# Adding the convolution's four channel chunks on VectorE before the mean product of an encoder layer

## The chip, the cores and the metric

The kernel runs on one core of a Trainium2 chip. The metric is the device time of one execution in microseconds (us); lower is better. The kernel before took 1318.83 us, the median of three runs that lay between 1318.5 and 1320.07 us.

## The reference

One encoder layer on 512 tokens of 1024 features. Two branches run on the normalised input and are joined by an output projection; a mixture of 32 experts (four for each token) follows, and a last norm. The part that the change touches is the layer norm of the convolution branch:

```
def conformer_conv(a, g, conv_w, conv_b, ln_g, ln_b):
    u = a * jax.nn.sigmoid(g)
    u = lax.conv_general_dilated(u, conv_w[:, None, :], ..., feature_group_count=D_CONV) + conv_b   # 31 taps, 512 channels
    uf = u.astype(jnp.float32)
    mu = jnp.mean(uf, axis=-1, keepdims=True)                   # over the 512 channels
    var = jnp.mean(jnp.square(uf - mu), axis=-1, keepdims=True)
    un = (uf - mu) * lax.rsqrt(var + EPS) * ln_g + ln_b
    return jax.nn.silu(un)
...
mixed = jnp.concatenate([conv_out, na_out], axis=-1)
return jnp.einsum("bse,ed->bsd", mixed, w_out) + b_out
```

The other branch, `na_out`, is attention with 8 heads of 64 over a neighbourhood of the 8 by 64 grid of tokens.

## The kernel before

The engines run programs of their own, written out by hand, and meet at semaphores. The work comes in stages: norm and input projection, convolution, attention, output projection, second norm and routing, then a loop over the experts, and the final sum and norm. The expert loop streams 12 pieces of 1 MB of weights for each expert; ScalarE and VectorE split each piece into a high and a low part, and TensorE multiplies. A piece's buffer is loaded again once TensorE has used it.

The convolution is done by VectorE. The 512 channels lie in four chunks of 128 partitions, `mixedT[:, c, :]`, each 128x512 f32. A tap is one instruction over a chunk (line 1190), 31 for each chunk, 124 in all. 88 of them are made before the attention; the last 36 lie two by two behind the scores of attention steps 0 to 17 (`TAP_STEPS`). The taps go round among the first two chunks that are not complete, and each waits for the one before it on its chunk.

The attention has 32 steps, `i` from 0 to 31: four blocks of 128 queries by 8 heads. In step `i`:

- VectorE (lines 1287 to 1314): `scores(i)` adds the bias table to the products and takes the row's extreme (line 1247); two taps; at steps 10, 18, 26 and 34 `normalise(n)` comes first, a reciprocal (line 1276) and a division of the block's output (line 1281), which waits for TensorE's value products `pv` of the 8 steps before. At steps 19 to 22 a chunk is centred (line 1302), which waits for `mean_done`.
- ScalarE: the exponential of step `i` (line 813) and the copy of the transposed weights (line 761).
- TensorE (lines 1911 to 1935): `transpose_p(i)` (line 1854), which waits for the exponential; in even steps `qk_pair(i + 4)`, the score products of two steps ahead (line 1844), which wait for `s_ready`; `pv(i - 1)` (line 1865). The first `pv` of a block waits for `normalise` of the block before (`o_ready`).

The mean over the channels is a product of a 128x128 matrix filled with 1/512 (`mean_w`) with each chunk, accumulated in bank 5 (line 1926), behind `pv` of steps 14, 15, 17 and 18. Each f32 product is two matmul instructions in the profile. `MEAN_OF` gives the places. Centring, squares (line 858, added up at line 1308), the product for the variance (line 1932) and the transposes of the next block's output at step 23 follow in this order. The output projection begins with `project_attn(1)` (line 1886) once the last `pv` is issued.

Of the kernel before, what the change touches and what calls it, by code (L numbers as in the profile page):

```python
# [10 lines left out]
ALU = mybir.AluOpType  # L11
# [18 lines left out]
CC = D_CONV // P  # L30
# [33 lines left out]
def encoder_kernel(nc, x, g_mix, w_in, b_in, conv_w, conv_b, ln_g, ln_b, rpb, w_out, b_out,  # L64
# [3 lines left out]
    with ctx:  # L68
        def sem(name):
            return ctx.enter_context(nc.semaphore(name))  # L70
# [10 lines left out]
        def area(name, shape, dt=F32):  # L81
            at = free[0]
            size = int(np.prod(shape[1:])) * (2 if dt == BF16 else 4)
            free[0] = at + -(-size // 128) * 128 if name == "area_u" else at + -(-size // 32) * 32
            return nc.alloc_sbuf_tensor_at(name, shape, dt, offset=at), at
# [10 lines left out]
        area_a, a_at = area("area_a", [P, 4096])  # L96
# [76 lines left out]
        mixedT = area_m[:, 0:2048].rearrange("p (k t) -> p k t", k=CC)  # L173
# [8 lines left out]
        mask = area_m[:, 3072:3072 + 768]  # L182
        sq = area_u[:, 0:2048].rearrange("p (b t) -> p b t", b=CC)
        ln_rs = area_a[:, 1024:1536]

        convT_out = [area_u[:, 512 * c:512 * (c + 1)] for c in range(CC)]
        T_mid = area_t[:, 0:2048].rearrange("p (h t) -> p h t", h=HEADS)
# [74 lines left out]
        mean_w, mean_at = area("mean_w", [P, P])  # L262
# [29 lines left out]
        bank = [pair[i // 2][:, 512 * (i % 2):512 * (i % 2 + 1)] for i in range(8)]  # L292
# [35 lines left out]
        conv_tap = sem("conv_tap")  # L328
        tables_ready = sem("tables_ready")
        mean_done = sem("mean_done")  # L330
        centred = sem("centred")
        squared = sem("squared")
        var_done = sem("var_done")
# [21 lines left out]
        attn_low_ready = sem("attn_low_ready")  # L355
# [96 lines left out]
        WOUT_PARTS = ((1, 2), (1, 3), (0, 2), (0, 3), (1, 0), (1, 1), (0, 0), (0, 1))  # L452
        TAP_STEPS = 18
        CENTRE_AT, SQUARE_AT, TURN_AT = 19, 20, 23
        MEAN_OF, SQUARES_AT, VAR_AT = {14: 0, 15: 1, 17: 2, 18: 3}, {23: (0, 1), 25: (2, 3), 27: (0, 2)}, 29
        next_tap, last_tap = [0] * CC, [0] * CC
        steps = [(n, hd) for n in range(NQ) for hd in range(HEADS)]
        NS = len(steps)
# [1 line left out]
        def normalised_at(i, first):  # L460
            return (i - first) // HEADS if i >= first and (i - first) % HEADS == 0 and (i - first) // HEADS < NQ else None

        def turned_at(i, behind):
            at = [10, TURN_AT, 26, 34]
            return at.index(i - behind) if i - behind in at else None
# [645 lines left out]
        def _(dve):  # L1111
            v = nc.vector
# [82 lines left out]
            def taps(count, known=CC):  # L1195

                for _ in range(count):
                    left = [c for c in range(known) if next_tap[c] < CONV_K]
                    tap(min(left[0:2], key=lambda c: last_tap[c]))
# [42 lines left out]
            def scores(i):  # L1242
                n, hd = steps[i]
                dve.wait_ge(qk_done, i + 2 - i % 2)
                if i >= 3:
                    dve.wait_ge(exp_ready, i - 2)
                v.tensor_tensor_reduce(out=S_sb[:, i % 3, :], in0=bank[i % 4][:, 0:KEYS], in1=table_of(n, hd),
                                       scale=1.0, scalar=3.0e38, op0=ALU.add, op1=ALU.min,
                                       accum_out=neg_max[:, i:i + 1]).then_inc(s_ready, 1)
# [8 lines left out]
            def attn_low_part(n):  # L1258
                tokens = slice(n * P, (n + 1) * P)
                dve.wait_ge(attn_high_ready, 4 * (n + 1))  # L1260
                for c in range(4):
                    v.scalar_tensor_tensor(attn_low[:, c, tokens], bank[5][:, c * P:(c + 1) * P], colT[:, 16 + c:17 + c],
                                           attn_high[:, c, tokens].bitcast(F32), ALU.add, ALU.subtract).then_inc(attn_low_ready, 1)
# [9 lines left out]
            def normalise(n):  # L1273

                dve.wait_ge(exp_ready, HEADS * (n + 1))
                v.reciprocal(row_inv[:, n * HEADS:(n + 1) * HEADS], row_sum[:, n * HEADS:(n + 1) * HEADS]).then_inc(inv_ready, 1)
                dve.wait_ge(inv_ready, n + 1)
                dve.wait_ge(pv_done, HEADS * (n + 1))
                if n:
                    dve.wait_ge(o_transposed, n)  # L1280
                v.tensor_tensor(O_sb.rearrange("p (h d) -> p h d", d=HEAD_DIM),
                                bank[7][:, :].rearrange("p (h d) -> p h d", d=HEAD_DIM),
                                row_inv[:, n * HEADS:(n + 1) * HEADS].unsqueeze(2).to_broadcast([P, HEADS, HEAD_DIM]),
                                ALU.mult).then_inc(o_ready, 1)

            WOUT_AT = {24: 0, 26: 1, 28: 2, 30: 3}
            for i in range(NS + 6):
                n = normalised_at(i, 10)
                if n is not None:
                    normalise(n)  # L1290
                if i < NS:
                    scores(i)
                if i < TAP_STEPS:
                    taps(2)
                n = turned_at(i, 3)
                if n is not None:
                    attn_low_part(n)
                if CENTRE_AT <= i < CENTRE_AT + CC:
                    c = i - CENTRE_AT
                    dve.wait_ge(mean_done, 1)  # L1300
                    dve.wait_ge(conv_tap, CONV_K * CC)
                    v.tensor_tensor(mixedT[:, c, :], mixedT[:, c, :], bank[5][:, :], ALU.subtract).then_inc(centred, 1)
                if i in SQUARES_AT:
                    a, b = SQUARES_AT[i]
                    dve.wait_ge(squared, max(a, b) + 1)
                    if (a, b) == (0, 2):
                        dve.wait_ge(var_summed, 2)
                    v.tensor_tensor(sq[:, a, :], sq[:, a, :], sq[:, b, :], ALU.add).then_inc(var_summed, 1)
                if i in WOUT_AT:
                    wout_low_part(WOUT_AT[i])  # L1310
                if i == NS + 3:
                    dve.wait_ge(std_ready, 1)
                    for q in range(4):
                        v.reciprocal(ln_rs[:, q * P:(q + 1) * P], ln_rs[:, q * P:(q + 1) * P]).then_inc(ln_rs_ready, 1)
# [423 lines left out]
            for k in range(11, NJ):  # L1738
                if k in ADD_AT:
                    i = ADD_AT.index(k)  # L1740
# [40 lines left out]
        def _(pe):  # L1781
            t = nc.tensor
            pe.wait_ge(consts_ready, 9)

            for n in range(NQ):
                pe.wait_ge(xn_ready, n + 1)
                for half in range(2):
                    i = 2 * n + half
                    if i >= 4:
                        pe.wait_ge(xnT_low_ready, i - 3)  # L1790
                    for c in range(4):
                        k = 4 * half + c
                        last = t.transpose(bank[4 + i % 4][:, c * P:(c + 1) * P], xn_tile[:, n % 2, k * P:(k + 1) * P], ident[:, :])
                    last.then_inc(xn_transposed, 1)
                if n == 0:
# [4 lines left out]
                    last = t.transpose(bank[0][:, 32:32 + rows], stage[0:rows, 1, :], ident[0:rows, 0:rows])  # L1800
# [11 lines left out]
            for g in range(16):  # L1812
# [9 lines left out]
                for k in range(KD):  # L1822
                    last = three_products(bank[g % 4][:, :], high[:, k, :], low[:, k, :], xnT_high[:, k, :], xnT_low[:, k, :], k)
# [87 lines left out]
            for i in range(NS + 5):  # L1911
                if i < NS:
                    transpose_p(i)
                if i % 2 == 0 and i + 4 < NS:
                    qk_pair(i + 4)
                if 1 <= i <= NS:
                    pv(i - 1)
                n = turned_at(i, 0)
                if n is not None:
                    transpose_o(n)  # L1920
                if i in MEAN_OF:
                    c = MEAN_OF[i]
                    pe.wait_ge(conv_tap, last_tap[c])
                    if c == 0:
                        pe.wait_ge(attn_low_ready, 4)
                    last = t.matmul(bank[5][:, :], mean_w[:, :], mixedT[:, c, :], start=(c == 0), stop=(c == CC - 1))
                    if c == CC - 1:
                        last.then_inc(mean_done, 1)
                if i == VAR_AT:
                    pe.wait_ge(var_summed, 3)  # L1930
                    pe.wait_ge(s_ready, NS - 3)
                    t.matmul(bank[0][:, :], mean_w[:, :], sq[:, 0, :], start=True, stop=True).then_inc(var_done, 1)
                if i == NS + 1:
                    pe.wait_ge(s_ready, NS)
                    project_attn(1)
# [43 lines left out]
            for n in range(NQ):  # L1979
                for m in range(n + 1):  # L1980
                    last = t.matmul(bank[0][:, n * 32:(n + 1) * 32], (before_b if m == n else ones_b)[:, :], chosen[:, m, :],
                                    start=(m == 0), stop=(m == n))
            for m in range(NQ):
                last = t.matmul(bank[0][:, NQ * 32:NQ * 32 + 32], ones_b[:, :], chosen[:, m, :], start=(m == 0), stop=(m == NQ - 1))
# [3 lines left out]
            for n in range(NQ):  # L1988
                last = t.matmul(bank[1][0:CAP, 0:2], first_pos[:, n, :], first_tok[:, n, :], start=(n == 0), stop=(n == NQ - 1))
# [4 lines left out]
                     start=True, stop=True).then_inc(sorted_turned, 1)  # L1994
# [247 lines left out]
```

## Time and profile before

| | |
|---|---|
| median of three runs | 1318.83 us (1318.5 to 1320.07) |
| the profiled execution | 1317.1 us |
| its span | 1315.4 us |
| TensorE matmul busy | 1257.9 us, 96% |
| VectorE busy | 1225.4 us, 93% |
| ScalarE busy | 967.1 us, 74% |
| GpSimd busy | 319.3 us, 24% |
| mean granted TensorE clock | 0.984 of full speed |
| the mean's products, line 1926 | 8 matmul instructions, 167.3 to 178.0 us |

The profiled execution is one run with the profiler on. Its span goes from the first to the last instruction; the 1.7 us that its time has beside the span lie around the program. Busy time is the time in which an engine has an instruction under way, and where a group of instructions is given, overlapping ones count once.

### The profile page before, as it was taken

What the parts mean: (1) busy time and instruction counts of PE and PEld (TensorE: products, weight loads), DVE (VectorE), ACT (ScalarE), POOL (GpSimd) and SP (SyncE); (2) the same over time, 40 slices, a digit from 0 to 9 for tenths busy, and PEclk for the clock granted to TensorE, in tenths of its full rate; (3) what the DMA queues carried; (4) which work ended last, traced back from release to release, by engine and by line L of the source; (5) the groups of instructions that cost most, each with busy time, mean ns of one, the idle gap of its engine ahead of it and who ended that gap; (6) DMA issues with size and microseconds to landing.
All of it is one profiled execution on the core that took longest, in us unless ns stands there. A gap on an engine that the chain in (4) does not pass through costs nothing.

```text
span 1315.4 us, 17620 instructions
## 1 busy us (share of the span) xinstructions
PE 1257.9 (96%) x5713; PEld 1001.4 (76%) x5713; DVE 1225.4 (93%) x1028; ACT 967.1 (74%) x788; POOL 319.3 (24%) x245
## 2 busy tenths in 40 slices
PE   4999889789999999999999999999999999999986
PEld 4887668667878778787778788887887878778764
DVE  6799976689999999999999999999999999999997
ACT  4241665358797979888878888888979797979761
POOL 6001000101132313141404141332323222313153
PEclk9999889979999999999999999999999999999999
DMA  9925791589999999999999999999999999999995
GB/s 285 389 80 145 272 367 37 206 312 410 391 422 404 423 410 416 411 414 419 410 408 409 422 410 420 412 421 411 421 409 422 410 421 411 421 411 422 406 388 166
DMA packets 89961, 481.60 MB, mean 366 GB/s; under 512 B 11017, under 2 KB 11316, under 8 KB 40774
## 3 DMA queue, kind: packets, MB, share of 16 engines
q1 hardware_dynamic: 77742, 448.89, 84.7%
q0 software_dynamic: 10400, 27.14, 6.1%
q10 hardware_dynamic: 1784, 5.14, 1.2%
q8 instruction: 18, 0.29, 0.1%
q14 instruction: 17, 0.14, 0.0%
HBM read 447.46 MB, written 41.66 MB: 372 GB/s over the span
## 4 chain that ended last, share of the span: by engine, by line
PE 77%; DVE 15%; issue 4%; ACT 2%; DMA 1%; POOL 0%; SPq 0%; DVEq 0%; ACTq 0%; POOLq 0%
PE pair L2026 13%; PE pair L2027 12%; PE pair L2028 12%; PE pair L2042 10%; PE pair L2043 10%; DVE w_low L1347 4%; DVE area_m L1190 4%; PE pair L2013 2%; PE pair L2006 2%; PE pair L2040 2%; PE pair L2049 2%; PE pair L2061 2%; PE pair L1807 1%; PE pair L1808 1%; PE pair L1809 1%
## 5 line engine op out<-in xcount | busy, mean ns | idle before, releaser
L1347 DVE TENSOR_TENSOR w_low<-w_raw,w_high 128x2048 fp32r<-128x2048 f32 x380 | 836.2, 2243 | 28.0 <-ACT w_high L885 26.1
L885 ACT CAST w_high<-w_raw 128x2048 fp32r<-128x2048 f32 x380 | 700.8, 1875 | 159.1 <-PE pair L2028 126.1
L2042 PE MATMUL pair<-w_high,xS 128*128 128x512 f32 x488 | 198.9, 408 | 0.4 <-DVE w_low L1581 0.2
L2026 PE MATMUL pair<-w_high,xT_high 128*128 128x512 f32 x480 | 192.4, 401 | 1.5 <-DVE w_low L1347 1.5
L2043 PE MATMUL pair<-w_low,xS 128*128 128x512 f32 x488 | 190.6, 391 | 0.0
L2027 PE MATMUL pair<-w_low,xT_high 128*128 128x512 f32 x480 | 188.0, 392 | 0.0
L2028 PE MATMUL pair<-w_high,xT_low 128*128 128x512 f32 x480 | 187.4, 390 | 0.0
L2026 PEld LDWEIGHTS pair<-w_high,xT_high 128*128 128x128 f32 x480 | 90.1, 188 | 30.9 <-DVE w_low L1347 6.7
L664 POOL DMA_INDIRECT y_rows<-area_m,place_now x30 | 104.9, 3497 | 28.1 <-issue 28.1
L2042 PEld LDWEIGHTS pair<-w_high,xS 128*128 128x128 f32 x488 | 91.7, 188 | 24.3 <-issue 4.2
L2043 PEld LDWEIGHTS pair<-w_low,xS 128*128 128x128 f32 x488 | 91.8, 188 | 21.9 <-issue 3.8
L642 POOL CAST sel_in<-is_expert 128x128 fp32r (+1 forms) x16 | 46.9, 2934 | 242.1 <-PE pair L2043 242.1
L2026 PE MATMUL pair<-w_high,hT_high 128*128 128x512 f32 x256 | 102.1, 399 | 3.3 <-DVE w_low L1347 3.3
L2028 PEld LDWEIGHTS pair<-w_high,xT_low 128*128 128x128 f32 x480 | 90.2, 188 | 19.6
L2027 PEld LDWEIGHTS pair<-w_low,xT_high 128*128 128x128 f32 x480 | 90.2, 188 | 17.4
L2028 PE MATMUL pair<-w_high,hT_low 128*128 128x512 f32 x256 | 100.5, 393 | 0.0
L2027 PE MATMUL pair<-w_low,hT_high 128*128 128x512 f32 x256 | 100.5, 392 | 0.0
L2042 PE MATMUL pair<-w_high,hS 128*128 128x512 f32 x240 | 95.0, 396 | 0.0
L2043 PE MATMUL pair<-w_low,hS 128*128 128x512 f32 x240 | 93.5, 390 | 0.0
L1190 DVE SCALAR_TENSOR_TENSOR area_m<-area_u,convT,area_m 128x512 f32<-128x512 f32 x120 | 83.6, 745 | 0.4
L629 POOL COPY tok_now<-tok_tab 128x1 int32 (+1 forms) x31 | 24.7, 796 | 186.6 <-PE pair L2006 84.7
L2026 PEld LDWEIGHTS pair<-w_high,hT_high 128*128 128x128 f32 x256 | 48.3, 189 | 14.8 <-issue 3.8
(376 smaller groups left out, 1871.4 us busy)
## 6 DMA issues: line engine op xcount, KB each, us to landing
w_raw<-in_w_gate SPq DMA_DIRECT2D x128, 1024.0 KB, 10.1
w_raw<-in_w_up SPq DMA_DIRECT2D x128, 1024.0 KB, 10.8
w_raw<-in_w_down SPq DMA_DIRECT2D x128, 1024.0 KB, 11.2
y_rows<-area_a SPq DMA_DIRECT2D x1, 15360.0 KB, 53.3
ring<-in_w_in SPq DMA_DIRECT2D x5, 2048.0 KB, 18.7
y_rows<-area_t SPq DMA_DIRECT2D x1, 9216.0 KB, 31.1
ring<-in_w_out SPq DMA_DIRECT2D x2, 2048.0 KB, 8.0
h<-in_x SPq DMA_DIRECT2D x4, 512.0 KB, 9.0
```

Source lines behind the costliest of these rows:

```text
L642: g.tensor_copy(sel_in[:, :], is_expert[:, bass.ds(e, 1)].to_broadcast([P, CAP])).then_inc(sel_in_ready, 1)
L664: g.indirect_dma_start(out=y_rows, out_offset=bass.IndirectOffsetOnAxis(ap=place_now[0:CAP - first_row, 0:1], axis=0), in_=y_sb[first_row: ...
L885: s.copy(w_high[:, i % HIGH_RING, raw:], w_raw[i][:, raw:]).then_inc(high_ready, 1)
L1190: v.scalar_tensor_tensor(mixedT[:, c, :], u_pad[:, c, k:k + SEQ], convT[:, k * CC + c:k * CC + c + 1], mixedT[:, c, :], ALU.mult, ALU.add) ...
L1347: v.tensor_tensor(w_low[i][:, raw:], w_raw[i][:, raw:], w_high[:, i % HIGH_RING, raw:].bitcast(F32), ALU.subtract).then_inc(low_ready, 1)
L2006: last = t.transpose(bank[6 + k // 4][:, (k % 4) * CAP:(k % 4 + 1) * CAP], xg[0:CAP, k::KD], ident[0:CAP, 0:CAP])
L2013: last = t.transpose(bank[6 + k // 4][:, (k % 4) * CAP:(k % 4 + 1) * CAP], h_tok[:, k::KD], ident[0:CAP, 0:CAP])
L2026: t.matmul(to[half], tok_high, hi, start=(opens and kk == 0), stop=False)
L2027: t.matmul(to[half], tok_high, lo, start=False, stop=False)
L2028: last = t.matmul(to[half], tok_low, hi, start=False, stop=(k == KD - 1))
L2042: t.matmul(to[half], rows, w_high[:, i % HIGH_RING, cols], start=(opens and kk == 0), stop=False)
L2043: last = t.matmul(to[half], rows, w_low[i if w is None else w][:, cols], start=False, stop=(k == KD - 1))
```

## The change

VectorE adds the four chunks into one, `chunk_sum`, 512 words that nothing else uses at that time. The addition of chunks 0 and 1 stands behind the taps of step 14, those of chunks 2 and 3 behind the taps of step 17. Each waits for the last tap of its chunk and, from the second on, for the addition before it (`mean_summed`). TensorE makes one product of `mean_w` with `chunk_sum` at step 18 in place of four at steps 14, 15, 17 and 18. It waits for the third addition. The mean is the same up to rounding.

```
+        chunk_sum = area_a[:, 1536:2048]
...
+        mean_summed = sem("mean_summed")
...
-        MEAN_OF, SQUARES_AT, VAR_AT = {14: 0, 15: 1, 17: 2, 18: 3}, {23: (0, 1), 25: (2, 3), 27: (0, 2)}, 29
+        CHUNKS_AT, MEAN_AT, SQUARES_AT, VAR_AT = {14: (1,), 17: (2, 3)}, 18, {23: (0, 1), 25: (2, 3), 27: (0, 2)}, 29
...
                 if n is not None:
                     attn_low_part(n)
+                for c in CHUNKS_AT.get(i, ()):
+                    dve.wait_ge(conv_tap, last_tap[c])
+                    if c > 1:
+                        dve.wait_ge(mean_summed, c - 1)
+                    v.tensor_tensor(chunk_sum, mixedT[:, 0, :] if c == 1 else chunk_sum, mixedT[:, c, :], ALU.add).then_inc(mean_summed, 1)
                 if CENTRE_AT <= i < CENTRE_AT + CC:
...
-                if i in MEAN_OF:
-                    c = MEAN_OF[i]
-                    pe.wait_ge(conv_tap, last_tap[c])
-                    if c == 0:
-                        pe.wait_ge(attn_low_ready, 4)
-                    last = t.matmul(bank[5][:, :], mean_w[:, :], mixedT[:, c, :], start=(c == 0), stop=(c == CC - 1))
-                    if c == CC - 1:
-                        last.then_inc(mean_done, 1)
+                if i == MEAN_AT:
+                    pe.wait_ge(mean_summed, CC - 1)
+                    pe.wait_ge(attn_low_ready, 4)
+                    t.matmul(bank[5][:, :], mean_w[:, :], chunk_sum, start=True, stop=True).then_inc(mean_done, 1)
```

## Rows read from the trace of the kernel before

**Rows 1.** Page, part 4: the chain that ended last, by engine.
```profile
PE 77%; DVE 15%; issue 4%; ACT 2%; DMA 1%; POOL 0%; SPq 0%; DVEq 0%; ACTq 0%; POOLq 0%
```

**Rows 2.** Busy time by engine in stretches, granted clock, DMA share, GB/s.
```profile
190.00:195.00 5.00, 4.72 (x25) 4.20 (x26) 3.21 (x11) 3.54 (x13) 0.00 (x0) 0.66 0.92 346
...
200.00:250.00 50.00, 50.00 (x252) 42.21 (x251) 33.69 (x44) 23.39 (x31) 2.96 (x8) 1.00 0.21 68
...
362.70:425.40 62.70, 62.70 (x284) 50.07 (x283) 60.58 (x33) 53.48 (x36) 17.41 (x10) 1.00 1.01 414
```

**Rows 3.** The chain that ended last, 165 to 178 us: start, us, what.
```profile
165.10 1.33 PE pair L1844 x8
166.44 1.04 PE pair L1865 x4
167.48 1.81 PE pair L1926 x2
169.29 0.43 PE pair L1854 x2
...
170.21 2.98 issue
...
174.66 0.91 PE pair L1926 x2
...
175.79 0.69 PE pair L1844 x8
176.49 0.59 PE pair L1865 x4
177.08 0.93 PE pair L1926 x2
```

**Rows 4.** Timeline: start, us, engine, line, operation, [idle before, releaser].
```profile
152.68 0.19 DVE L1276 RECIPROCAL area_m<-area_m 128x8 f32<-128x8 f32 x1
152.95 0.69 DVE L1281 TENSOR_TENSOR area_a<-pair,area_m 128x512 f32<-128x512 f32 x1
...
158.90 1.41 DVE L1190 SCALAR_TENSOR_TENSOR area_m<-area_u,convT,area_m 128x512 f32<-128x512 f32 x2
...
167.27 2.02 PE L1926 MATMUL pair<-area_m,mean_w 128*128 128x512 f32 x2
...
168.55 1.53 DVE L1190 SCALAR_TENSOR_TENSOR area_m<-area_u,convT,area_m 128x512 f32<-128x512 f32 x2
...
170.00 0.20 DVE L1276 RECIPROCAL area_m<-area_m 128x8 f32<-128x8 f32 x1
...
170.26 1.34 PE L1926 MATMUL pair<-area_m,mean_w 128*128 128x512 f32 x2
...
173.19 0.69 DVE L1281 TENSOR_TENSOR area_a<-pair,area_m 128x512 f32<-128x512 f32 x1 [2.99 <-issue]
...
174.99 0.14 PEld L1854 LDWEIGHTS pair<-ident,area_m 128*128 128x128 f32 x1 [0.24 <-ACT area_m L813]
...
178.03 0.69 DVE L1302 TENSOR_TENSOR area_m<-area_m,pair 128x512 f32<-128x512 f32 x1 [3.46 <-PE pair L1926]
...
181.80 0.69 DVE L1308 TENSOR_TENSOR area_u<-area_u 128x512 f32<-128x512 f32 x1
...
182.40 0.42 DVE L1247 CUSTOM_DVE_ANT_0 area_m<-pair,ring 128x256 f32<-128x256 f32 x1
...
199.37 0.48 PE L1886 MATMUL pair<-wout_high,attn_high 128*128 128x512 f32 x1
```

**Rows 5.** Busy time by engine in 1 us slices, granted clock before DMA share.
```profile
162.00:163.00 1.00, 0.70 (x6) 0.65 (x6) 1.00 (x5) 0.51 (x3) 0.00 (x0) 1.00 1.04 408
163.00:164.00 1.00, 0.27 (x3) 0.14 (x2) 0.96 (x4) 0.71 (x3) 0.00 (x0) 0.98 1.06 412
164.00:165.00 1.00, 0.63 (x2) 0.23 (x2) 1.00 (x4) 1.00 (x2) 0.00 (x0) 0.50 1.04 408
...
170.00:171.00 1.00, 1.00 (x4) 0.70 (x4) 0.20 (x2) 1.00 (x3) 0.00 (x0) 0.61 1.04 408
```

## The prediction

> **What bounds the kernel now.** I read the page first, then the chain that ended last, then the busy time in equal stretches, and only then the instructions around the edit. The chain is mostly TensorE's [rows 1], but the share says nothing of one stage, so the reader should look at the stretches [rows 2]. From 200 us to 250 us TensorE is busy for all 50 us, and in the expert loop all of a stretch of 62.70 us, some two experts long, is busy as well. What starts that work is the end of the attention stage, and everything behind it (projection, norm, routing, experts) follows it in one piece. So a microsecond gained or lost before about 199.4 us, where the first product of the output projection starts [rows 4], should be passed on to the end in full. The weight loads don't stop this: they are started by semaphores that TensorE's own use of the buffers raises.
>
> Inside the attention stage no engine is full. The chain of the stretch around the edit [rows 3] goes to and fro: TensorE's score and value products, then the mean's first product (1.81 us of the chain), then 2.98 us that the chain calls issue and that end in VectorE's `normalise(1)`, then TensorE again with two more of the mean's products (0.91 and 0.93 us). The last one releases the first centring. Its row [rows 4] says that VectorE stood idle 3.46 us before it, released by line 1926. So the mean's products are on the path that sets the end, at least the last two.
>
> **What goes.** Eight matmul instructions (two for each of the four products) become two. One product costs 2.02 us of TensorE at the first place and 1.34 at the second; of the last two the chain holds 0.91 and 0.93 [rows 3, 4]. The difference is the granted clock: it is at half (1.2 GHz) from 164 us until some way into the slice from 170 to 171, and full (2.4 GHz) behind it [rows 5]. The first three go: 2.02 + 1.34 + 0.91 = 4.27 us of TensorE time, of which only a part is on the path.
>
> **What comes.** Three additions of 128x512 f32 on VectorE. The trace has this form with both inputs in SBUF at line 1308: 0.69 us long, and the next instruction starts 0.60 us after it started (181.80 to 182.40, [rows 4]). The first addition stands behind step 14's taps and waits for chunk 1, whose last tap (number 71) is long past; chunks 0 and 1 were done before the attention began and chunk 2 at step 13, counting the taps from the code. So it costs 0.60. Behind step 17 the addition of chunk 2 costs 0.60. That of chunk 3 must wait for its result, and what such a wait costs shows in the taps: two on different chunks take 1.41 us together, two on one chunk, where the second needs the first, take 1.53 [rows 4]. So I take 0.60 + 0.12 = 0.72. Together 0.60 + 0.60 + 0.72 = 1.92 us. The rule that speaks for a higher price stands in the Trainium skill, VectorE: DVE Perf Modes, section The DRAIN you can't avoid: the next operation doesn't start until the pipe is empty. By it three times 0.69 = 2.07 us would be paid, 0.15 us more; the row with its start 0.60 later says otherwise for instructions that don't depend on each other.
>
> The waits added on VectorE are on its own results, and behind them stand the scores of step 15 and `normalise(1)`; for these ScalarE's exponentials wait. TensorE's one wait, at step 18, is for the third addition, which by the count below is done about 4 us before. It costs nothing; without that cover it would cost at most the same 1.92.
>
> **The sum, step by step.** Step 14's addition pushes the scores of steps 15, 16 and 17 back by 0.60. TensorE's score products at step 14 wait for the scores of step 15 (165.10), so they start at 165.70. From there at the half clock: 1.33 for the score products, 1.04 for the values, no mean, 0.43 for the transposes, 1.04 values, 0.43 transposes, 1.33 or less for score products, 1.04 or less for step 15's values [rows 3]. That is 165.70 + 6.64 = 172.3 if all is at half clock, and about 171.6 if the clock rises in the slice from 170 to 171, as it did. Before, the division of `normalise(1)`, which waits for them, began at 173.19 [rows 4].
>
> VectorE: the reciprocal of `normalise(1)` started at 170.00 [rows 4]. It is pushed by 1.92 to 171.9, and the division follows 0.27 later where nothing is awaited (152.68 to 152.95): 172.2. Taking the later of the two engines, between 172.2 and 172.4, I use 172.3: 0.9 us earlier than 173.19. So the additions lie for the most part in the 2.98 us that VectorE waited.
>
> From there: the trace has 1.80 us from the start of the division (173.19) to the load of step 18's transposes (174.99, behind ScalarE's exponential). In the old kernel those transposes were held until the mean's third product ended at 174.66 + 0.91 = 175.57 [rows 3]. Now they follow at once: 172.3 + 1.80 = 174.1, then 0.43 for the transposes, 0.69 for score products, 0.59 for values, 0.93 for the one mean product, which ends at 176.7. Before, the last product ended at 177.08 + 0.93 = 178.0. The difference is 1.3 us; the early end of the two that `normalise(1)` allows is 172.2 and the late one 172.4, and since the semaphores of the new waits have a price too, I take 1.2.
>
> Behind that the order of work is unchanged, so the sum is -1.2 us. The profiled execution took 1317.1 us (span 1315.4, and 1.7 around it), which would become 1315.9. It lies 1.7 under the median of the three timed runs, so I apply the difference to that median: 1318.83 - 1.2 = 1317.6 us. For a measurement of this kernel, whose three runs lie 1.57 us apart, a change counts as one from 0.2%, which is 2.64 us.
>
> **Bounds of what I can't see.** A floor for the time is that VectorE's two waits (2.98 and 3.46) go away whole and only the additions are paid: 6.44 - 1.92 = 4.5 us gained, 1314.3. A ceiling without a change of clock is that all additions are on the path and neither wait shrinks: +1.9, 1320.7.
>
> **Rivals.**
>
> The clock falls (25%). In the old kernel the granted clock was full from 171 to about 191 us. Around 163 to 164 us it fell, and what TensorE did before that was little: busy 0.70 and 0.27 of the two microseconds [rows 5]. In the new kernel TensorE has such a poor stretch of its own: after step 15's values at 171.6 or so, one pair of transposes and one pair of value products until 174.1. If the clock then falls, the steps before the centring cost 0.43 + 1.33 + 1.04 + 1.81 = 4.6 us [rows 3] in place of 2.64, so +2.0, and the sum turns to +0.8: 1319.6 us. The Trainium skill has this as a rule, TensorE: Matmul & The Clock Gate, section Why this matters for your kernels: idle gaps between bursts of matmuls bring the clock back to its half rate. By the rule taking products out of a thin stretch can cost more than it saves; by the old trace the clock stayed full through VectorE's waits of 2.98 and 3.46 us, in which TensorE had gaps too. I hold the full clock to be likelier, because TensorE works without a gap up to 171.6 and again from 174.1.
>
> The gain is not passed on, or there is none (10%). If `normalise(1)` starts when it did, only the third product's hold on the transposes goes (their load at 174.99 against 175.57 [rows 3, 4]): -0.6, 1318.2 us. Or a later wait swallows it: then 0. Against: TensorE is full from 200 us on.
>
> Faster by more than 0.2% (12%). The clock was at half also around 191 to 194 us ([rows 2], 0.66 over 190 to 195) where TensorE was busy 4.72 of 5 us. If the shifted work misses that fall, up to half of about 3.4 us of work at half clock comes back: -1.2 - 1.7 = -2.9, 1315.9 us.
>
> Slower by more than 0.2% (6%). The clock falls at about 174 us as in the first rival and stays at half as long as it did from 164 until it rose in the slice from 170 to 171 [rows 5], some 6.6 us, so until 180.6. The one product then ends near 178.7, and of the next 1.9 us as much as is TensorE's work on the chain takes twice its time: up to +1.9 beyond the +0.8, so +2.7, 1321.5 us. It decides once the half clock covers more than 1.8 us of chain work behind the mean, for then 2.64 is passed.
>
> The forecast case has what is left, 47%; its own range is 1316.9 to 1318.3.
>
> **How the numbers follow.** Forecast, clock rival and no-gain rival are all within 0.2%: 0.82. Faster 0.12, slower 0.06. The range must take in the clock rival at 1319.6 and its spread to 1320.7 (the ceiling above), and on the low side the faster case's near edge, 1315.9. So 1315.9 to 1320.7; that leaves out the slow rival and the rest of the fast one.
>
> **What would show it.** Right: two matmuls at the mean's line; three additions of 0.69 us; `normalise(1)`'s division about 0.9 us earlier with its wait shrunk from 2.99 us to a few tenths; the first centring near 176.8 us with an idle time before it of about 2 us; TensorE's first projection product 1.2 us earlier than 199.4. Wrong: a granted clock of 0.50 anywhere between 174 and 182 us, or a centring near 178 us in spite of the shorter mean, or a shift at 199.4 us that isn't found again at 250.

## The result, and the profile after

The changed kernel is slower: 1323.20 us, the median of 17 runs (1317.69 to 1328.16), against 1317.53 us for the kernel before beside it (17 runs, 1315.36 to 1324.01). The ratio is 1.0035 with a 95% interval of 1.0023 to 1.0047. The forecast was 1317.6 us, which is 1.2 us less than before, the range 1315.9 to 1320.7, and "slower by more than 0.2%" had a chance of 0.06. The medians lie 5.7 us apart the other way.

The page of the changed kernel's profiled execution (1324.54 us, span 1322.8): busy time of the engines, then TensorE's busy share and granted clock in 40 equal slices of 33 us.

```profile
PE 1264.9 (96%) x5707; PEld 1007.3 (76%) x5707; DVE 1227.1 (93%) x1031; ACT 967.7 (73%) x788; POOL 319.9 (24%) x245
...
PE   4999899979999999999999999999999999999986
...
PEclk9999959979999999999999999999999999999999
```

Six matmuls fewer and three VectorE instructions more, as the diff says, yet TensorE is busy 7.0 us longer (1264.9 against 1257.9). The reason stands in the last row: the sixth slice, 165 to 198 us, has a granted clock of 0.5, where the kernel before had 0.8. The busy time of TensorE in three stretches, granted clock in the column before the DMA share; first the changed kernel, then the kernel before.

```profile
164.00:171.00 7.00, 6.22 (x33) 5.66 (x34) 6.79 (x15) 3.70 (x11) 0.00 (x0) 0.50 1.05 410
171.00:191.00 20.00, 18.75 (x77) 13.62 (x75) 8.73 (x27) 10.67 (x33) 0.00 (x0) 0.50 1.05 403
191.00:200.00 9.00, 7.31 (x32) 5.84 (x30) 6.31 (x18) 4.11 (x16) 0.00 (x0) 0.50 0.37 141
```

```profile
164.00:171.00 7.00, 6.53 (x23) 4.58 (x24) 6.09 (x14) 3.78 (x10) 0.00 (x0) 0.52 1.05 409
171.00:191.00 20.00, 15.47 (x105) 10.70 (x104) 12.85 (x37) 12.95 (x43) 0.00 (x0) 1.00 1.05 402
```

Read the middle rows together. In the same 20 us the old kernel got through 105 matmuls in 15.47 us of busy time, the new one through 77 in 18.75 us. The engine that looks busier did less: it ran at 1.2 GHz. In slices of 1 us the new kernel's clock is at 0.50 from 164 us to 204 us without a break; in the old kernel it came back in the slice from 170 to 171 [rows 5].

The chain that ended last through the same steps as [rows 3] (start, us, what):

```profile
169.68 0.70 DVE area_a L1304
...
172.14 1.08 PE pair L1872 x4
173.23 0.49 PE pair L1861 x2
173.72 1.26 PE pair L1851 x8
174.98 1.04 PE pair L1872 x4
176.02 1.83 PE pair L1931 x2
```

And the instructions that answer to [rows 4], from the timeline (line 1304 is the new addition, 1283 the division of `normalise(1)`, 1309 the first centring, 1931 the one mean product):

```profile
161.91 0.41 DVE L1249 CUSTOM_DVE_ANT_0 area_m<-pair,area_t 128x256 f32<-128x256 f32 x1
...
163.69 0.69 DVE L1304 TENSOR_TENSOR area_a<-area_m 128x512 f32<-128x512 f32 x1
...
169.68 1.48 DVE L1304 TENSOR_TENSOR area_a<-area_a,area_m 128x512 f32<-128x512 f32 x2
...
170.42 0.63 PE L1872 MATMUL pair<-area_t,area_a 128*128 128x64 f32 x2
...
171.08 0.20 DVE L1278 RECIPROCAL area_m<-area_m 128x8 f32<-128x8 f32 x1
171.31 0.69 DVE L1283 TENSOR_TENSOR area_a<-pair,area_m 128x512 f32<-128x512 f32 x1
...
175.81 2.02 PE L1931 MATMUL pair<-area_a,mean_w 128*128 128x512 f32 x2
...
177.87 0.69 DVE L1309 TENSOR_TENSOR area_m<-area_m,pair 128x512 f32<-128x512 f32 x1 [5.19 <-PE pair L1931]
```

The division starts at 171.31, 1.9 us earlier than in the old kernel, with no wait ahead of it where 2.99 us stood. The centring starts at 177.87 against 178.03: level. The loss comes behind it. The first output-projection product starts at 199.37 us in the old kernel [rows 4] and at 205.5 in the new one. How that travels to the end, by the first and last start of three lines (router and the last residual products); the changed kernel first, then the kernel before:

```profile
L1893 PE MATMUL pair<-wout_high,attn_high x32: 389/389/481, 205.5 to 227.2; 128*128 128x512 f32 x32
...
L1963 PE MATMUL pair<-area_t,area_q x32: 270/275/275, 251.9 to 256.3; 128*128 128x128 f32 x32
...
L2200 PE MATMUL pair<-h,ident x8: 590/592/697, 1307.2 to 1312.1; 128*128 128x512 f32 x8
```

```profile
L1960 PE MATMUL pair<-area_t,area_q x32: 270/275/276, 245.4 to 249.7; 128*128 128x128 f32 x32
...
L2197 PE MATMUL pair<-h,ident x8: 591/592/697, 1300.8 to 1305.7; 128*128 128x512 f32 x8
```

The shift is 6.1 us at the projection, 6.5 at the router, 6.4 at the last products; the last 1.0 of the 7.4 us in the span comes behind these. What is lost before 205 us is passed on through 1100 us of experts.

### The profile page after: what moved, and what is told of

It is laid out like the page before. It is cut to its first block, busy times and chain, and to the rows that moved or that the text cites. A ratio compares the mean times of both kernels' runs of the same rounds, so it can differ in the third digit from the quotient of the medians.

```text
span 1322.8 us, 17613 instructions
## 1 busy us (share of the span) xinstructions
PE 1264.9 (96%) x5707; PEld 1007.3 (76%) x5707; DVE 1227.1 (93%) x1031; ACT 967.7 (73%) x788; POOL 319.9 (24%) x245
## 4 chain that ended last, share of the span: by engine, by line
PE 75%; DVE 15%; issue 4%; ACT 3%; DMA 2%; POOL 0%; DVEq 0%; SPq 0%; ACTq 0%; POOLq 0%
PE pair L2029 13%; PE pair L2030 12%; PE pair L2031 12%; PE pair L2045 10%; PE pair L2046 10%; DVE w_low L1354 4%; DVE area_m L1192 4%; PE pair L2016 2%; PE pair L2009 2%; PE pair L2043 2%; PE pair L2052 2%; PE pair L2064 1%; PE pair L1814 1%; PE pair L1815 1%; DVE h L1709 1%
```

## The experiments

Each was timed beside the kernel before, whose medians were 1315.91, 1316.41, 1315.70 and 1315.88 us in the four sets. The times of some kernels fall in two groups, so I give the single runs' spread where it matters. Steps, banks and names are those of the kernel section.

### Products back, and additions away

e1 puts three products back whose results nobody reads, and keeps the additions:

```
+        WARM_AT = {14: 0, 15: 1, 17: 2}
...
+                if i in WARM_AT:
+                    if i == min(WARM_AT):
+                        pe.wait_ge(attn_low_ready, 4)
+                    pe.wait_ge(conv_tap, last_tap[WARM_AT[i]])
+                    t.matmul(bank[5][:, :], mean_w[:, :], mixedT[:, WARM_AT[i], :], start=True, stop=True)
```

> The changed kernel with three products of the mean matrix put back at steps 14, 15 and 17, whose results are overwritten and unused; the additions on VectorE stay. Theory (the clock): the three products were what brought the granted clock back up at 170.6 us in the old trace, and with them the clock is full again for most of 171 to 191 us; the time is within 1.5 us of the kernel before. Rival (the additions lie on the path): the additions are all still there, so the time stays 4 to 5 us above the kernel before, and more by the products.

e2 drops the additions and lets the one product take chunk 3 alone:

```
-                for c in CHUNKS_AT.get(i, ()):
...
-                    pe.wait_ge(mean_summed, CC - 1)
+                    pe.wait_ge(conv_tap, last_tap[3])
                     pe.wait_ge(attn_low_ready, 4)
-                    t.matmul(bank[5][:, :], mean_w[:, :], chunk_sum, ...
+                    t.matmul(bank[5][:, :], mean_w[:, :], mixedT[:, 3, :], ...
```

> The changed kernel without the three additions: the one product at step 18 takes chunk 3 alone, so the mean leaves out three chunks. Theory (the clock): TensorE's load is that of the changed kernel, the clock stays at half from about 163 us to the output projection, and the time is 3 to 5 us above the kernel before although VectorE has less to do than in either kernel. Rival (the additions): without them the time falls to or below that of the kernel before, by 1 to 2 us.

Measured: e1 1317.13 us (12 runs, 1314.89 to 1325.72; ratio 1.0022, 1.0009 to 1.0035), e2 1322.33 us (7 runs; 1.0036, 1.0023 to 1.0050). With all the additions and the old products the median is 1.2 us above the kernel before; with none of the additions and one product it is 6.4 above. The stretch from 171 to 191 us, e1 and then e2:

```profile
171.00:191.00 20.00, 15.47 (x97) 10.88 (x97) 14.43 (x41) 12.65 (x41) 0.00 (x0) 0.93 1.05 402
```

```profile
171.00:191.00 20.00, 18.91 (x77) 13.58 (x75) 8.63 (x26) 10.67 (x33) 0.00 (x0) 0.50 1.04 402
```

e2's row is the changed kernel's, less an instruction of VectorE. The rival that the additions cost the time falls: they can be taken out and the loss stays. What the products give back isn't settled by this pair alone, for the intervals of e1 and e2 overlap; the next two runs settle it.

### How many products, and where

e5 and e6 are e1 with fewer products: `WARM_AT = {14: 0, 15: 1}` and `WARM_AT = {14: 0}`.

> The changed kernel with two unused products put back, at steps 14 and 15. Theory (the clock): these two are the products that lay ahead of the clock's rise at 170.6 us in the old trace, so the clock rises again as in e1, the first centring comes near 176 us, and the time is that of e1 or up to 1 us less. Rival (the whole of the old load is needed, not its place): the clock stays at half as in the changed kernel and the time is 5 us or more above the kernel before.

> The changed kernel with one unused product put back, at step 14. Theory (the clock): the share of executions in which the clock rises lies between e5 and the changed kernel, so a median between them and a spread at least as wide. Rival (only the product at step 15 matters): as the changed kernel.

Measured: e5 1316.72 us (12 runs; ratio 1.0007, 0.9992 to 1.0021), e6 1316.77 us (11 runs; 1.0006, 0.9997 to 1.0015). One unused product of the mean matrix at step 14 takes the loss away: both intervals lie under the changed kernel's (1.0023 to 1.0047), with all three additions still there. I had expected e6 between e5 and the changed kernel; it is as good as e5. Its eleven runs lie between 1313.03 and 1318.94. The clock of its profiled execution (1318.34 us, one of its longer ones), in two stretches:

```profile
168.00:172.00 4.00, 4.00 (x23) 3.19 (x21) 2.74 (x5) 2.08 (x5) 0.00 (x0) 0.57 1.05 410
172.00:176.00 4.00, 3.04 (x22) 2.44 (x21) 1.38 (x5) 2.56 (x7) 0.00 (x0) 0.85 1.05 409
```

It comes back in the slice from 171 to 172, falls once more at about 175 and is full again from 179 to 188.

e15 keeps the old load, adds nothing on VectorE, and moves all four products of the kernel before to step 18:

```
-        MEAN_OF, ... = {14: 0, 15: 1, 17: 2, 18: 3}, ...
+        MEAN_OF, ... = {18: 0}, ...
...
+                    for c in range(CC):
+                        last = t.matmul(bank[5][:, :], mean_w[:, :], mixedT[:, c, :], start=(c == 0), stop=(c == CC - 1))
```

> The kernel before with all four mean products moved to step 18: TensorE's load is the old one, nothing is added on VectorE, only the place differs. Theory (the clock, and it is the products ahead of 171 us that bring it up): the steps 14 to 17 are as thin as in the changed kernel, so the clock stays at half up to step 18 and the centring is late by 2 us or more; the four products in a row there bring the clock up, so the time lies 2 to 4 us above the kernel before and seldom at 7. Rival (the total of TensorE work decides): the time of the kernel before, plus at most the 1 to 2 us by which the products are bunched. Second rival (the additions): no more than 2 us, since there are none.

Measured: 1320.08 us (5 runs, 1319.82 to 1322.21; ratio 1.0036, 1.0023 to 1.0050). Two stretches of its profile, and what the first centring waited for (us, times):

```profile
171.00:178.00 7.00, 7.00 (x23) 4.49 (x24) 0.32 (x2) 2.56 (x7) 0.00 (x0) 0.50 1.05 408
178.00:191.00 13.00, 10.61 (x65) 7.05 (x63) 9.09 (x28) 8.63 (x29) 0.00 (x0) 0.96 1.04 397
...
  PE pair L1925: 9.1, 1
```

The four products start at 174.45 us and take 5.92 us in a row. The clock is at half until 179, when some three quarters of that time is over, and full from there to 192: 8 us later than in the kernel before. Same work, other place, 4.2 us more, a little over the 2 to 4 expected and over both rivals. So the total of the work doesn't decide. How much of the 4.2 us is the bunching can't be told from this run: the centring comes at 180.4 in place of 178.0, the first projection product at 202.6 in place of 199.4.

Nine profiled executions have no filling products. In slices of 1 us, the first slice behind 165 us in which the granted clock is above 0.50 is:

| with a product of the mean matrix at step 14 | without one there |
|---|---|
| kernel before 170, e1 167, e5 169, e6 171, e11 (below) 168 | e12 (below) 178, e15 179, changed kernel 204, e2 204 |

The two groups don't overlap. Each is one execution, so this shows where the clock comes back, not how often.

e11 is the version half way: one addition (chunks 0 and 1, behind step 10's taps) and three products.

```
-        MEAN_OF, ... = {14: 0, 15: 1, 17: 2, 18: 3}, ...
+        MEAN_OF, ... = {14: 0, 15: 2, 18: 3}, ...
...
+                if i == 10:
+                    dve.wait_ge(conv_tap, last_tap[1])
+                    v.tensor_tensor(chunk_sum, mixedT[:, 0, :], mixedT[:, 1, :], ALU.add).then_inc(mean_summed, 1)
...
+ mean_w[:, :], chunk_sum if c == 0 else mixedT[:, c, :], start=(c == 0), ...
```

> The kernel before with one addition on VectorE, chunks 0 and 1 behind step 10's taps, and three products in place of four, at steps 14, 15 and 18; the mean is whole. Theory (the clock): the two products at 14 and 15 bring the clock up, one product of 1.08 us is gone from the path to the centring, 0.6 us of VectorE is added: from 1 us below to the time of the kernel before. Rival (any product fewer lets the clock fall): 4 us or more above it.

Measured: 1318.37 us (12 runs; ratio 1.0020, 1.0004 to 1.0036), and neither expectation was right. Eight runs lie between 1315.26 and 1319.51 with a mean granted clock of 0.980 or more, four between 1322.8 and 1323.4 with 0.972 or 0.973. One program, two outcomes. The profile is of one of the four (1323.13 us):

```profile
172.00:176.00 4.00, 3.04 (x23) 2.36 (x23) 1.37 (x5) 2.56 (x7) 0.00 (x0) 0.96 1.05 409
176.00:180.00 4.00, 3.42 (x12) 1.87 (x10) 2.50 (x8) 1.43 (x5) 0.00 (x0) 0.50 1.05 409
```

The clock came back in the slice from 168, as the theory had it, fell again in the slice from 175, and was at half until 189 and from 193 to 203; the projection starts at 204.6. So with products at steps 14 and 15 the clock came back early, and the loss came from the next fall. e5 has its mean products at the same steps and only one of its 12 runs above 1320 us. Whether the places of the additions or chance separate the two is not shown.

### The same kernel, two outcomes

e12 is the changed kernel again.

> The changed kernel once more, beside the others on the same chip. Theory (the clock): 4 to 6 us above the kernel before at a granted clock of about 0.972 in most executions, and about 1 to 3 us above it in the few in which the clock is 0.976 or more. Rival (chance of the chip on which it was timed): within 1.5 us of the kernel before.

Measured: 1318.81 us (8 runs; ratio 1.0039, 1.0022 to 1.0056), 3.1 us above the kernel before. Three of the eight took 1323.59 to 1324.57, five 1316.35 to 1318.92, so the long ones were not the most of them, as I had expected, and the rival's 1.5 us is passed too. Its profiled execution took 1318.70 us, and its clock differs from that of the first profile of the very same program:

```profile
164.00:171.00 7.00, 6.23 (x33) 5.66 (x34) 6.79 (x15) 3.70 (x11) 0.00 (x0) 0.50 1.05 410
171.00:178.00 7.00, 6.35 (x25) 4.39 (x24) 1.77 (x8) 2.56 (x7) 0.00 (x0) 0.50 1.05 410
178.00:191.00 13.00, 9.64 (x64) 6.76 (x62) 11.50 (x34) 9.52 (x33) 0.00 (x0) 0.89 1.04 397
```

Here the clock came back in the slice from 178 us, right behind the one mean product, and was at half again from 189 to 199; the first projection product starts at 200.8 us. Both executions centre at 177.9. So the difference between the two outcomes, 4.7 us at the projection, is the clock behind the centring. Over the 25 runs of this kernel the mean granted clock sorts the times: 13 runs at 0.973 or less took 1322.75 to 1328.16 us, 5 runs at 0.976 or more took 1316.35 to 1319.25, and 7 between lie in both groups. Of the kernel before, 4 of 113 runs in the four sets were above 1320 us, and 4 of the 17 in the comparison of the result. The median of a kernel like this moves with the share of executions in each group, which is why e12's median is 4.4 us under the first one while the ratios agree.

### Filling: the version that beats both

e4 is the kernel before with one unused bf16 product of 512 columns ahead of each step's transposes, written to the bank that the transposes then overwrite; e3 is the changed kernel with the same.

```
+            def fill(i):
+                if i >= 2:
+                    pe.wait_ge(pT_ready, i - 1)
+                t.matmul(bank[PT_BANKS[i % 2]].rearrange("p (a e) -> p a e", a=4), ones_b[:, :],
+                         ones_b[:, :].unsqueeze(1).to_broadcast([P, 4, P]), start=True, stop=True)
...
             def transpose_p(i):
+                if FILL_FROM <= i:      # FILL_FROM = 2
+                    fill(i)
```

> The changed kernel with one bf16 product of 512 columns ahead of the transposes of each attention step from step 2 on, where TensorE mostly waits for ScalarE; it writes the bank that the transposes then overwrite, and nothing reads it. Theory (the clock): the clock stays full through the attention, and the changed kernel falls to 3 us or more below the kernel before. Rival (the additions): the clock may rise, but the change's cost stays, and the time is at best that of the kernel before.

> The kernel before with the same bf16 products. Theory (the clock): the full clock gives back what the three stretches at half clock cost, 2 to 5 us below the kernel before; and beside e3, where the clock is full too, it shows what the change is worth by itself: e3 should be about 1.2 us faster than this one. Rival (the additions): e3 is slower than this one by 2 us or more.

e7 and e8 are e3 and e4 with the product twice.

> The changed kernel with two bf16 products of 512 columns a step from step 2 on. Theory (the clock): twice the filling holds the clock at full for more of 150 to 200 us than in e3 (0.50 from 168 to 180 us there), and the time comes down from e3's 1318.6 to at most that of the kernel before. Rival (TensorE's own time becomes the bound): some 30 products more at 0.21 us each cost what the clock gives, and the time is that of e3 or above.

> The kernel before with two bf16 products a step. Theory (the clock): no stretch at half clock is left, and the time is 1 us or more under e4; beside e7 it shows what the change is worth at full clock (e7 1.2 us faster, if the prediction's sum holds). Rival (TensorE's own time): e4's time or above.

e13 is e3 with one mean product back at step 14, e14 is e4 again.

> The changed kernel with one bf16 product of 512 columns in each step and one unused f32 product at step 14. Theory (at equal clock the change is worth its sum): the time is 1 us or more under the kernel before with the same filling (e14), whose median was 1314.3 in e4. Rival (the change is worth nothing at any clock): the time of e14 or above it.

> e4's kernel again, beside e13 on one chip. Theory (the clock): 1 to 2 us under the kernel before, as in e4. Rival (chance): no difference from the kernel before.

Medians, with the ratio to the kernel before:

| | kernel before, filled | changed kernel, filled |
|---|---|---|
| once | e4 1314.26, 0.9991 (0.9983 to 1.0000) | e3 1318.59, 1.0023 (1.0012 to 1.0034) |
| once, second set | e14 1313.38, 0.9983 (0.9974 to 0.9992) | e13 (one back) 1314.97, 0.9993 (0.9984 to 1.0002) |
| twice | e8 1316.76, 1.0005 (0.9994 to 1.0015) | e7 1317.92, 1.0012 (0.9999 to 1.0025) |

The kernel before with one filling product a step is the fastest here, 1.7 and 2.5 us under the plain one at mean granted clocks of 0.982 to 0.989 against 0.978 to 0.985. Twice as many cost what they give: e8 lies 0.4 us above the kernel before where e4 lay 1.7 below, as its rival had it, and e7 comes down from 2.7 us above to 1.5, but not to the kernel before. In none of the three pairs is the changed kernel ahead.

Measured against what I expected: e4 fell a little short of its 2 to 5 us, and e14, the same kernel, went a little beyond its 1 to 2; e3, e7 and e13 all missed. e3 is 4.3 us above e4, which is what the rivals of both (the additions) had said, and e13 is above e14, as its rival had it. But e3's clock isn't full: its profile has 0.50 from 167 to 180 us, and e7's from 166 to 175, while e8's is full from 150 to 188. So none of the three is a pair at equal clock, and they don't tell the additions from the clock; e2 and e6 do. Only e3 and e4 are clearly apart; the intervals of e7 and e8, and of e13 and e14, overlap.

e9 and e10 put two such products only in even steps 4 to 18, ahead of the score products.

```
+                if i in FILL_AT:        # range(4, 20, 2)
+                    pe.wait_ge(pT_ready, i)
+                    for _ in range(2):
+                        t.matmul(bank[PT_BANKS[(i + 1) % 2]]..., ones_b[:, :], ones_b broadcast to 512 columns, start=True, stop=True)
                 if i % 2 == 0 and i + 4 < NS:
                     qk_pair(i + 4)
```

> The kernel before with two bf16 products of 512 columns in even steps 4 to 18 only, placed ahead of the score products, where TensorE waits for VectorE's scores. Theory (the clock): fewer stretches at half clock between 153 and 171 us, at less cost than filling every step, so the time is that of e4 or below, some 2 us under the kernel before. Rival (the filling's cost eats it): no change from the kernel before.

> The changed kernel with the same filling as e9. Theory (the clock): the products make up for the missing ones at steps 14 to 17 and the clock rises before the centring; the time falls by 4 us or more against the changed kernel, to that of the kernel before. Rival (bf16 products don't count as the f32 ones do): the time stays with the changed kernel.

Measured: e9 1316.81 us (11 runs; ratio 1.0010, 1.0001 to 1.0018), e10 1322.21 us (10 runs; 1.0040, 1.0022 to 1.0057). e9's rival was right: the filling gives nothing. e10 has the two groups again: four runs from 1315.15 to 1317.81, six from 1321.85 to 1325.12. In the six these bf16 products don't stand in for the f32 ones, though there are sixteen of them. The profile is of one of the four. It and e9's happen to have the same clock up to the centring, which makes them the fair pair for the prediction's sum. e9, then e10:

```profile
152.38 0.69 DVE L1282 TENSOR_TENSOR area_a<-pair,area_m 128x512 f32<-128x512 f32 x1
...
177.10 0.69 DVE L1303 TENSOR_TENSOR area_m<-area_m,pair 128x512 f32<-128x512 f32 x1 [3.89 <-PE pair L1932]
...
164.00:171.00 7.00, 7.00 (x30) 4.48 (x28) 4.01 (x10) 2.79 (x7) 0.00 (x0) 0.62 1.05 409
171.00:178.00 7.00, 5.96 (x40) 3.99 (x38) 2.28 (x7) 2.57 (x7) 0.00 (x0) 1.00 1.05 409
```

```profile
152.41 0.69 DVE L1284 TENSOR_TENSOR area_a<-pair,area_m 128x512 f32<-128x512 f32 x1
...
175.00 0.69 DVE L1310 TENSOR_TENSOR area_m<-area_m,pair 128x512 f32<-128x512 f32 x1 [3.45 <-PE pair L1937]
...
164.00:171.00 7.00, 6.31 (x36) 5.00 (x35) 6.70 (x15) 3.12 (x10) 0.00 (x0) 0.63 1.05 410
171.00:178.00 7.00, 5.59 (x37) 3.75 (x37) 3.55 (x14) 4.50 (x14) 0.00 (x0) 1.00 1.05 406
```

From the division of `normalise(0)` to the first centring: 24.72 us with four products, 22.59 with the change. At equal clock the change gains 2.1 us there. The gain is still there at the first projection product, 198.0 us against 200.3: behind the centring the clock is at half for some 10 us in either (187 to 196 in e10, 190 to 200 in e9).

## Why the prediction was wrong

It forecast 1.2 us less and the medians are 5.7 us apart the other way. Two of its three signs of being wrong came: a clock of 0.50 between 174 and 182 us, and a centring near 178 us (177.87) in spite of the shorter mean.

**The additions: right.** Step 14's scores start at 161.91 in the new profile and at 162.83 in the old one: the new execution came there 0.92 us ahead. The reciprocal starts at 171.08 against 170.00, 1.08 behind. So the additions cost 2.00 us of VectorE; 1.92 was forecast. By the rule of the Trainium skill that was weighed there (VectorE: DVE Perf Modes, section The DRAIN you can't avoid) it would have been 2.07; the measurement lies between, and the next instruction starts 0.60 us after the first addition does (163.69 to 164.29), as the row at line 1308 had said. They hid in the 2.98 us wait, as forecast: the division has no idle time ahead of it.

**The first half of the sum: right.** Step 15's values end at 171.05 (170.42 + 0.63); between 171.6 and 172.3 was forecast. The division starts at 171.31 instead of 172.3. Of these 1.0 us the new execution had brought 0.92 along.

**The clock: the step that failed.** "I hold the full clock to be likelier, because TensorE works without a gap up to 171.6 and again from 174.1." The clock never came back at 171: it was at 0.50 before and after. The first rival's price for that was good. It said 4.6 us in place of 2.64 for the steps from the transposes to the product's end; the chain has 0.49 + 1.26 + 1.04 + 1.83 = 4.6. The error was to set 25% on it and to look for a second fall at 174 us, where in truth the rise at 170 to 171 hung on the products that the diff removes. The prediction's sum took those products out and kept the clock that had come with them. e6 shows this in one edit: one of them back, unused, and the median is 0.4 us from the kernel before. The second fall that the rival priced does exist: e6 and e11 have it at about 175 us, after a rise before it.

**How long the clock stays at half: mis-sized.** The sum put nothing for the clock behind the centring ("the order of work is unchanged"). The slow rival let it stay at half for 6.6 us and ended at +2.7. It stayed for 40 us, from 164 to 204. From the centring to the projection, 21.3 us became 27.6, which is 6.3 us, and with the centring level this is the whole loss. The old trace had shown the half clock for some 6.6 us at most, and I took this for its natural length. What ended it differs from run to run. In e12, the same program, the clock came back right behind the one mean product of step 18; in this execution that product (175.81 us) changed nothing, and the rise at 204 stands behind the variance's product, the next one with the mean matrix:

```profile
201.39 2.02 PE L1935 MATMUL pair<-area_u,mean_w 128*128 128x512 f32 x2
```

The rule of the Trainium skill that the first rival named (TensorE: Matmul & The Clock Gate, section Why this matters for your kernels: gaps between bursts bring the clock down) gave the right sign, but the measurement goes further than gaps: in the changed kernel TensorE was busy 18.75 of 20 us at the half clock and stayed there.

**Passing on to the end: right** for a shift of this size, 6.1, 6.5 and 6.4 us at three places. A single microsecond can't be followed so: from the router's first product to the last residual products' first the seventeen profiles take between 1053.7 and 1056.1 us.

**Whether the change could pay.** At equal clock up to the centring it gains 2.1 us in one pair of profiles (e9, e10), more than the 1.2 of the sum. As medians the gain isn't seen in any of three filled pairs, where the changed kernel is 4.3, 1.2 and 1.6 us behind. Nor were their clocks equal. Picked out afterwards by the mean granted clock, at 0.989 and 0.990, three runs of e7 took 1315.90 to 1316.53 us and four of e8 1316.70 to 1317.56, about 1 us in favour of the change; e13 and e14 show no such gain. So a gain of 1 to 2 us at equal clock is suggested, not shown. I can't say which steps behind the centring decide how long the clock is at half there, and no run isolates it. Open too is what sorts the executions of one program into the two groups; the trace shows the clock that results, not why it fell that way.

## What to carry to other kernels

In a stage of many small products the granted clock is part of the balance: before counting a removed dense product as saved time, look at which products lie just ahead of a rise of the clock in the old trace, and price the stage to its end at the half clock. Busy share doesn't warn of it, since the same small work at half clock looks busier; read the matmul count beside the busy time. Look at single runs, not at the median alone: two groups of times with two mean clocks are the sign.

## What was not expected of the hardware

- TensorE stayed at half clock for 40 us while it was busy 0.94 of a 20 us stretch (18.75 of 20) with transposes, score products and value products of 64 to 256 columns and one 512-column product of the mean matrix (175.81 to 177.83 us).
- One f32 product of the mean matrix (128x512, two matmul instructions, about 2 us at the half clock) at step 14 was enough to bring the distance of the medians from 5.7 us to 0.4; sixteen bf16 products of 512 columns in even steps were not in six of ten runs (e10), and thirty, one a step, left 2.7 us (e3).
- The same program ran in two groups about 5 us apart, sorted by the mean granted clock: 0.973 and less, or 0.976 and more. In two profiled executions of it TensorE's work and clock agree from 164 to 178 us, and only then does the clock come back in one of them.
